# A hybrid decoder layer on one core: four PSUM banks, packed gate weights and GpSimd multiplies in the prologue

## Time and profile before

| | us |
|---|---|
| time, median of 3 runs | 1647.21 |
| lowest and highest run | 1644.97 and 1647.9 |
| span of the profiled execution | 1645.5 |
| PE busy | 1612.2 |
| DVE busy | 881.7 |
| ACT busy | 645.3 |
| POOL busy | 121.1 |

### The profile page before, as it was taken

The page is one execution under the profiler, slowest core; times in us unless marked ns, Lnnn a source line. Parts: engine busy times, 40 slices in busy tenths (PEclk is TensorE's granted clock), DMA queues, the critical chain, the costliest instruction groups (busy, mean ns, idle before and its releaser), DMA issues.

```text
span 1645.5 us, 22286 instructions
## 1 busy us (share of the span) xinstructions
PE 1612.2 (98%) x8376; PEld 1372.1 (83%) x8376; DVE 881.7 (54%) x1511; ACT 645.3 (39%) x1090; POOL 121.1 (7%) x228
## 2 busy tenths in 40 slices
PE   6999999999999999999999999999999999999998
PEld 5788888888888788898888888888888888888886
DVE  6444444444444543663244474555555567676876
ACT  5445555455554642341132342433334331212123
POOL 0000000000000000000000002333333320000000
PEclk9999999999999899999999999999999999999999
DMA  5101010011110142151210213666666799676753
GB/s 191 49 26 28 16 39 15 26 28 28 27 28 14 62 127 82 44 162 51 64 39 1 65 51 122 223 218 215 217 209 210 257 365 351 230 273 206 262 204 154
DMA packets 153103, 204.76 MB, mean 124 GB/s; under 512 B 8208, under 2 KB 93328, under 8 KB 153008
## 3 DMA queue, kind: packets, MB, share of 16 engines
q1 hardware_dynamic: 135104, 144.95, 27.2%
q0 software_dynamic: 17920, 58.73, 10.2%
HBM read 140.61 MB, written 63.57 MB: 124 GB/s over the span
## 4 chain that ended last, share of the span: by engine, by line
PE 92%; DVE 3%; ACT 3%; issue 1%; DMA 0%; SPq 0%; DVEq 0%
PE psG L741 16%; PE psG L724 11%; PE psG L726 11%; PE psG L725 11%; PE psS L1129 9%; PE psO L921 7%; PE psO L1129 5%; PE psG L1129 5%; PE psS L851 3%; PE psG L827 3%; PE psS L753 2%; PE psS L752 2%; PE psG L1051 2%; PE psG L1053 2%; PE psG L1052 2%; PE psS L769 1%
## 5 line engine op out<-in xcount | busy, mean ns | idle before, releaser
L724 PE MATMUL psG<-act_hi,w_hi 128*128 128x512 f32 x640 | 249.3, 389 | 0.0
L726 PE MATMUL psG<-act_hi,w_lo 128*128 128x512 f32 x640 | 249.0, 389 | 0.0
L725 PE MATMUL psG<-act_lo,w_hi 128*128 128x512 f32 x640 | 249.0, 389 | 0.0
L921 PEld LDWEIGHTS psO<-V,pT 128*128 128x128 f32 x1152 | 147.0, 192 | 16.8 <-ACT pT L1241 6.7
L710 POOL DMA_DIRECT2D op_rows<-a_hi x112 | 60.6, 541 | 1228.6 <-DVE a_lo L1431 1193.3
L741 PE MATMUL psG<-act_hi,w_lo 128*128 128x512 f32 x360 | 150.4, 418 | 0.0
L741 PE MATMUL psG<-act_hi,w_hi 128*128 128x512 f32 x360 | 148.2, 412 | 0.0
L921 PE MATMUL psO<-V,pT 128*128 128x64 f32 x1152 | 144.6, 271 | 2.7 <-ACT pT L1241 2.6
L741 PE MATMUL psG<-act_lo,w_hi 128*128 128x512 f32 x360 | 145.3, 404 | 0.0
L1241 ACT ACTIVATE pT<-psS 128x128 f32<-128x128 f32 (+7 forms) x128 | 79.9, 625 | 160.7 <-PE psS L851 160.6
L725 PEld LDWEIGHTS psG<-act_lo,w_hi 128*128 128x128 f32 x640 | 120.1, 188 | 25.0
(11 more groups left out here) (238 smaller groups left out, 3152.2 us busy)
## 6 DMA issues: line engine op xcount, KB each, us to landing
act_hi<-op_rows SPq DMA_DIRECT2D x38, 1024.0 KB, 7.3
op_rows<-a_hi POOLq DMA_DIRECT2D x112, 256.0 KB, 2.8
op_rows<-a_lo POOLq DMA_DIRECT2D x112, 256.0 KB, 3.3
act_lo<-op_rows SPq DMA_DIRECT2D x18, 1024.0 KB, 7.5
raw<-in_w_up_dram SPq DMA_DIRECT2D x32, 512.0 KB, 4.7
raw<-in_w_in_dram SPq DMA_DIRECT2D x22, 512.0 KB, 4.0
qB<-in_w_down_dram SPq DMA_DIRECT2D x8, 1024.0 KB, 9.9
act_late<-in_w_down_dram SPq DMA_DIRECT2D x8, 1024.0 KB, 10.7
```

The source lines that it names most:

```text
L724: nc.tensor.matmul(dst, sh, mh, start=(k == 0), stop=False)
L725: nc.tensor.matmul(dst, sh, ml, start=False, stop=False)
L726: mm = nc.tensor.matmul(dst, sl, mh, start=False, stop=(k == n - 1))
L921: mm = nc.tensor.matmul(psO[:, u % 2, 0:HEAD], pT[:, b * P:(b + 1) * P], V[par][:, b, h * HEAD:(h + 1) * HEAD], start=(b == 0), stop=(b == ...
```

## The change

- **Banks.** The first tiles are summed in four banks, the two of `psG` and the two of `psO` (`FIRST_BANKS`); `FIRST_FREED` names the tile that each later one waits for. The thrown-away squares go to an SBUF tile `first_sq` at the place where `gate_lo` was.
- **Gate.** The low parts of the 8 gate columns are written into columns 32 to 39 of each 128-wide block of `gate_hi`, and the gate's high part is split by ACT at t = 7. A gate tile is then 16 matmuls: each block by the high and by the low activations. The result has the high columns' sums on partitions 0 to 7 and the low columns' on 32 to 39; ACT copies the latter to `gate_e`, and DVE adds both and the bias.
- **GpSimd.** POOL multiplies tiles 1 to 7 by `a_gain` as they arrive, into four buffers `a_hn`; DVE multiplies the result in place by the reciprocal root, with a `tensor_scalar`. Tile 0 stays as it was. POOL also subtracts for the low parts of the Q and the K weight tile, after its tiles 5 and 7.

```diff
-    gate_lo = at("gate_lo", [P, 1024], f32r, 186)
+    first_sq = at("first_sq", [P, D], f32, 186)
...
-    a_hn = [at(f"a_hn{i}", [P, D], f32, 166 + 4 * i) for i in range(2)]
+    a_hn = [at(f"a_hn{i}", [P, D], f32, kb) for i, kb in enumerate((166, 170, 134, 138))]
...
+        FIRST_BANKS = (psG[0][:], psG[1][:], psO[:, 0, :], psO[:, 1, :], psG[0][:], psO[:, 1, :], psO[:, 0, :], psG[1][:])
+        FIRST_FREED = (None, None, None, None, 0, 3, 2, 1)
+        GATE_LOW = 32
...
         @block.gpsimd
         def _(pool):
+            pool.wait_ge(gain_loaded[0], 16)
+            for t in range(1, TT):
+                pool.wait_ge(x_loaded[t], 16)
+                if t >= 4:
+                    pool.wait_ge(n_tr, t - 3)
+                nc.gpsimd.tensor_tensor(a_hn[t % 4][:], X[:, t, :], a_gain[:], ALU.mult).then_inc(x_gained, 1)
+                if t in (5, 7):
+                    i = 1 if t == 5 else 2
+                    hi, lo = (None, (w_hi[1], w_lo[1]), first_k)[i]
+                    pool.wait_ge(hi_done, i + 1)
+                    nc.gpsimd.tensor_tensor(lo[:], raw_first[i - 1][:], hi[:].bitcast(f32), ALU.subtract).then_inc(lo_done, 1)
...
+            def gate_tile(j, half):
+
+                tok = slice(half * HALF, (half + 1) * HALF)
+                for k in range(KT):
+                    both = gate_hi[:, k * P:(k + 1) * P]
+                    nc.tensor.matmul(FIRST_BANKS[j], both, act_hi[:, k, tok], start=(k == 0), stop=False)
+                    mm = nc.tensor.matmul(FIRST_BANKS[j], both, act_lo[:, k, tok], start=False, stop=(k == KT - 1))
+                mm.then_inc(tile_done, 1)
+
...
-                if j >= 2:
-                    pe.wait_ge(tile_out, j - 1)
+                if FIRST_FREED[j] is not None:
+                    pe.wait_ge(tile_out, FIRST_FREED[j] + 1)
...
             for i in range(2):
+                pe.wait_ge(tile_out, (1, 6)[i])
                 v_transposes(i, i)
...
-                    sq(t, X[:, t, :], (x_loaded[t], 16))
+                    sq(t, X[:, t, :], (x_loaded[t], 16), squares=first_sq[:])
...
-            split_hi(gate_hi[:], gate_raw[:], gate_hi_done, (gate_loaded, 16))
-
-            def qk_hi_out(j, chunk, half, a, heads=(0, 1), done=qk_hi):
+                if t == 7:
+                    split_hi(gate_hi[:], gate_raw[:], gate_hi_done, (gate_loaded, 16))
...
+                if chunk == GATE_:
+                    act.wait_ge(tile_done, j + 1)
+                    nc.scalar.activation(gate_e[:, half * HALF:(half + 1) * HALF], FIRST_BANKS[j][GATE_LOW:GATE_LOW + 8, :],
+                                         ACT.Copy).then_inc(gate_low, 1)
...
-                    if t >= 3:
-                        dve.wait_ge(n_tr, t - 2)
-                    norm_scale(t - 1, X[:, t - 1, :], a_hn[(t - 1) % 2], a_gain, (gain_loaded[0], 16))
+                    norm_chain(t - 1)
+                    dve.wait_ge(x_gained, t - 1)
+                    hn = a_hn[(t - 1) % 4][:]
+                    nc.vector.tensor_scalar(hn, hn, rstd[:, (t - 1) % 2:(t - 1) % 2 + 1], None, ALU.mult).then_inc(n_hn, 1)
...
-                if t in (3, 5, 6):
-                    i = max(0, t - 4)
-                    block_lo(i, i, (raw[0], *raw_first)[i], first_k if i == 2 else None)
+                if t == 3:
+                    block_lo(0, 0, raw[0])
...
-            dve.wait_ge(gate_hi_done, 1)
-            lo_part(gate_lo[:], gate_raw[:], gate_hi[:], gate_lo_done)
+                if t == TT - 1:
+                    dve.wait_ge(gate_hi_done, 1)
+                    both = gate_hi[:].rearrange("p (k n) -> p k n", n=P)
+                    lo_part(both[:, :, GATE_LOW:GATE_LOW + 8], gate_raw[:].rearrange("p (k n) -> p k n", n=P)[:, :, 0:8],
+                            both[:, :, 0:8], gate_lo_done)
...
-                    nc.vector.tensor_scalar(gate_z[:, half * HALF:(half + 1) * HALF], psG[j % 2][0:8, :], b_col[:], None,
-                                            ALU.add).then_inc(tile_out, 1)
+                    cols_z = slice(half * HALF, (half + 1) * HALF)
+                    dve.wait_ge(gate_low, half + 1)
+                    nc.vector.scalar_tensor_tensor(gate_z[:, cols_z], FIRST_BANKS[j][0:8, :], b_col[:], gate_e[:, cols_z],
+                                                   ALU.add, ALU.add).then_inc(tile_out, 1)
```

More of the change, by code:

```diff
@@ L329, in hybrid_layer @@
         gate_lo_done = sem("gate_lo_done")
+        gate_low = sem("gate_low")
         gate_act = sem("gate_act")
@@ L364, in hybrid_layer @@
         n_hn = sem("n_hn")
+        x_gained = sem("x_gained")
         n_tr = sem("n_tr")
@@ L731, in col_block, with proj @@
                 return slot_hi[:, k * P:(k + 1) * P], slot_lo[:, k * P:(k + 1) * P]
-            def proj(j, chunk, half, r0, r1, slots):
+            def proj(j, chunk, half, r0, r1, slots, dst=None):
+                dst = psG[j % 2][:] if dst is None else dst
                 for r in range(r0, r1):
@@ L740, in proj @@
                     a, b = ((hi, mh), (hi, ml), (lo, mh))[part]
-                    mm = nc.tensor.matmul(psG[j % 2][:], a, b, start=(r == 0), stop=(r == 23))
+                    mm = nc.tensor.matmul(dst, a, b, start=(r == 0), stop=(r == 23))
                     if r == 23:
@@ L774, in _ @@
             for t in range(TT // 2 - 1):
-                norm_tr(t, a_hn[t % 2])
+                norm_tr(t, a_hn[t % 4])
             def first_tile(part, k0=0, k1=KT):
@@ L790, in _ @@
             first_tile(0, 0, 5)
-            norm_tr(TT // 2 - 1, a_hn[1])
+            norm_tr(TT // 2 - 1, a_hn[3])
             first_tile(0, 5, KT)
-            slots = [(w_hi[0], w_lo[0]), (w_hi[1], w_lo[1]), first_k, (gate_hi, gate_lo)]
+            slots = [(w_hi[0], w_lo[0]), (w_hi[1], w_lo[1]), first_k]
+            def gate_tile(j, half):
[5 more added lines that the diff above has]
+                mm.then_inc(tile_done, 1)
             for j, (chunk, half) in enumerate(FIRST_TILES):
@@ L802, in _ @@
                     pe.wait_ge(gate_lo_done, 1)
-                if j >= 2:
-                    pe.wait_ge(tile_out, j - 1)
+                if FIRST_FREED[j] is not None:
+                    pe.wait_ge(tile_out, FIRST_FREED[j] + 1)
                 if j in (1, 2):
-                    proj(j, chunk, half, 0, PRODUCTS // 2, slots)
-                    norm_tr(TT // 2 + 2 * j - 1, a_hn[1])
-                    proj(j, chunk, half, PRODUCTS // 2, PRODUCTS, slots)
+                    proj(j, chunk, half, 0, PRODUCTS // 2, slots, FIRST_BANKS[j])
+                    norm_tr(TT // 2 + 2 * j - 1, a_hn[(2 * j - 1) % 4])
+                    proj(j, chunk, half, PRODUCTS // 2, PRODUCTS, slots, FIRST_BANKS[j])
+                elif chunk == GATE_:
+                    gate_tile(j, half)
                 elif j:
-                    proj(j, chunk, half, 0, PRODUCTS, slots)
+                    proj(j, chunk, half, 0, PRODUCTS, slots, FIRST_BANKS[j])
                 else:
@@ L813, in _ @@
                 if j < 2:
-                    norm_tr(TT // 2 + 2 * j, a_hn[0])
+                    norm_tr(TT // 2 + 2 * j, a_hn[2 * j % 4])
             for i in range(2):
+                pe.wait_ge(tile_out, (1, 6)[i])
                 v_transposes(i, i)
@@ L1178, in _, with qk_hi_out @@
                     split_hi((w_hi[1], first_k[0])[i][:], raw_first[i][:], hi_done, (raw_first_loaded[i], 16))
-            split_hi(gate_hi[:], gate_raw[:], gate_hi_done, (gate_loaded, 16))
-            def qk_hi_out(j, chunk, half, a, heads=(0, 1), done=qk_hi):
+                if t == 7:
+                    split_hi(gate_hi[:], gate_raw[:], gate_hi_done, (gate_loaded, 16))
+            def qk_hi_out(j, chunk, half, a, heads=(0, 1), done=qk_hi, bank=None):
                 tok = slice(half * HALF, (half + 1) * HALF)
+                bank = psG[j % 2][:] if bank is None else bank
                 for h in heads:
-                    src = psG[j % 2][h * HEAD:(h + 1) * HEAD, :]
+                    src = bank[h * HEAD:(h + 1) * HEAD, :]
                     places = (qhl[a][h][0:HEAD, tok], qb_[a][h][0:HEAD, tok]) if chunk == Q_ else \
@@ L1194, in _ @@
                     act.wait_ge(tile_done, j + 1)
-                    qk_hi_out(j, chunk, half, 0)
+                    qk_hi_out(j, chunk, half, 0, bank=FIRST_BANKS[j])
+                if chunk == GATE_:
+                    act.wait_ge(tile_done, j + 1)
+                    nc.scalar.activation(gate_e[:, half * HALF:(half + 1) * HALF], FIRST_BANKS[j][GATE_LOW:GATE_LOW + 8, :],
+                                         ACT.Copy).then_inc(gate_low, 1)
                 if chunk == V_ and half == 1:
@@ L1436, in norm_var, with norm_chain @@
                 nc.vector.tensor_scalar(neg_var4[:, i], sum_sq[:, i], -4.0 / D, -4.0 * EPS, ALU.mult, ALU.add).then_inc(n_var, 1)
-            def norm_scale(n, src, dst, gain_t, *waits, column_parts=(slice(0, D),)):
+            def norm_chain(n):
                 i = slice(n % 2, n % 2 + 1)
```

(16 more changed lines are left out.)

## The result

The changed kernel takes 1650.59 us (median of 18 runs) against 1647.78 us before: 2.8 us more, a ratio of 1.0022 with a 95% interval of 1.0015 to 1.0029. The forecast was 1642.3 us in a range of 1637.8 to 1651.5. The time lies in the range, and on the wrong side: rival B, priced at 1651.1 us, is what happened.

The account below looks back on a forecast made before the run. PE, busy 98% of the span, was taken as the bound. Span 1645.5 us, -8.1 for banks and gate, +3.2 for the front (sum -4.9), +1.7 around the span: 1642.3 us, range 1637.8 to 1651.5.

Parts of the forecast that it names:

- rival B: Front: every two-input VectorE instruction, one-column ones too, waits out GpSimd: about +12 us, 1651.1 us in all; chance 0.19.
- Parts 1 and 2: Four banks and packed gate in the prologue: less idle PE, slow clock and gate matmuls, -8.1 us together.
- the hole: PE idle for 3 us between K tile and gate, slow clock behind; four banks should save 3.15 and 1.59 us.
- rival C: Late drains hold the second V tile, so the hole and its slow clock come back there: 1646.9 us; chance 0.14.
- part 3: GpSimd's multiplies and weight splits in the front: hardly shorten PE's path, full-width VectorE instructions take turns, +3.2 us.
- front term: Prologue before the gate: delay of PE from VectorE taking turns with GpSimd, +3.2 us, bounds -1 and +12.
- Rival A: Front: VectorE and GpSimd run side by side without turns, nothing lost there: 1639.1 us, down to 1637.8; chance 0.25.
- B's third piece: Front, last weight split: 1.3 us of the about +12 us that rival B claimed.

Follow-up runs that it names:

- experiment 1: Changed kernel with GpSimd's loop taken out and VectorE normalising and splitting as before, four banks and packed gate kept: 1639.34 us.
- experiment 4: experiment 1 plus nine GpSimd multiplies whose products VectorE and PE never wait for: 1649.93 us.
- experiment 3: Changed kernel with the two one-column instructions of each norm chain taking their second vector as a scalar operand: 1641.52 us.
- experiment 5: experiment 1 plus nine GpSimd memsets of 128 by 2048 into unused tiles, which only write SBUF: 1639.01 us.
- experiment 6: experiment 3 with an unread row sum added to VectorE's normalising multiply, meant to take it to single rate: 1640.52 us.

## Why the prediction was wrong

**Parts 1 and 2 were right to the size**: -8.1 us forecast, -8.1 measured in experiment 1. No wait took the hole's place there, and the softplus chain and V's copies stayed clear, so rival C falls.

**GpSimd's instruction was near**: 2.2 us assumed, 2.38 measured, and 1.97 in the mean for experiment 4, where both operands are the same tile. Its nine instructions, some 21 us, did fit between 8 and 45 us. The estimate from the Trainium skill (GPSIMD Engine Reference, section "Elementwise — side-by-side cycle accounting"), 2.25 us, was as near.

**The failed step is in part 3: "I take the middle: the full-width instructions (multiply, weight split) take turns with GpSimd, the one-column ones don't."** I reasoned by how many elements an instruction moves. What counts is how many operands it takes from SBUF: an instruction of one element per partition with two of them waits out a GpSimd instruction as one of 1024 elements does (1.89, 2.26 and 2.80 us in a row). Each tile's chain has two of these one-column instructions ahead of the multiply, so where GpSimd has work queued, three of its instructions pass for one tile instead of one. The front term was mis-sized for that: +3.2 us forecast, 11.6 us measured (54.14 against 42.54), made up for the most part as rival B had it: 5.8 us at the first projection and still at the second part of the V tile (24.07 against 18.32, 30.88 against 25.08), and 4.20 us of idle PE at tile 4. Most of the remaining 1.6 us is the slow clock behind that idle stretch. From tile 4's transposes to tile 5's PE takes 5.07 us in the changed kernel (38.21 to 43.28, with the granted clock of 0.66 above), and for the same matmuls in the kernel before 3.62 us:

```profile
28.05 1.04 PE L769 MATMUL psS<-ident,a_hn 128*128 128x128 f32 x8
...
31.67 1.03 PE L769 MATMUL psS<-ident,a_hn 128*128 128x128 f32 x8
```

That is 1.45 us which no term of the prediction has. B's third piece, 1.3 us at the last split, cost PE nothing: from 38.21 to the gate PE waits for no tile. So it is in part luck that B's total of 12 us came so near: the slow clock, which B left out, made up for the piece that cost nothing. With the two one-column instructions freed of the second operand, the forecast's number came out, and nearly its path (experiment 3). Rival A falls with experiments 3 and 4.

The trace of before held a hint that I read too weakly: 0.68 us for one operand against 1.22 for two pointed to a second way into SBUF. The Trainium skill (SBUF — State Buffer, section "Who interferes with whom") says that a VectorE instruction with two SBUF inputs and a GpSimd instruction that reads SBUF exclude each other, but not one that only writes, and that VectorE at its double rate and GpSimd exclude each other too, a rate that the form of tensor_scalar that also writes out its accumulator doesn't take. The runs agree: 1.89 us with two operands and 0.27 with one (experiment 3), no stretched row beside memsets (experiment 5), 1.28 us each with the accumulator (experiment 6). I gave that rule, taken to the letter, 0.19.

## What to carry to other kernels

Before moving elementwise work to GpSimd, list VectorE's instructions beside it by where their operands come from, and don't leave out the tiny ones: a chain of one-column instructions with two tensor operands can cost one whole GpSimd instruction each. Giving the second operand of such a one-column instruction as a per-partition scalar took it out of GpSimd's way here (0.27 and 0.21 us). Of the full-width instructions, the one with one of its two operands in PSUM was not held up (1.22 us), and the multiply with a single operand still was (1.88 us). And ask first whether the engine that is relieved sets the end in that stage: the prediction argued that VectorE hardly does here, and no version with GpSimd's multiplies beat experiment 1 without them, 1639.34 us.

## What was not expected of the hardware

The exclusion costs GpSimd too: its multiplies have a mean of 2.38 us in the changed kernel and of 2.76 us in experiment 3, where VectorE's full-width instructions come between more often (2.34 us the shortest; 3.36 us the one from 18.61 on, beside the V weight split at 17.92). And in the profile such a wait looks like a slow instruction, not like a wait; a group whose mean is well above its own shortest instruction is the sign to look for.
